# Decoder layer on one core: the moving tiles of the split matmuls start 32 or 96 bytes past a multiple of 128

## The reference

```
mod = (silu(c) @ w_ada + b_ada)                      # 9 vectors of 1024
h = modulate(rms_norm(x, g1), shift, scale)
x = x + 0.5 * gate * (silu(h @ w_gate) * (h @ w_up)) @ w_ffn1_out     # D_FF = 2816
h = modulate(rms_norm(x, g2), ...)
u_pool, q_lat, kv_lat, k_rope, g_pool, g_mla = split(h @ w_in)
br_pool = (causal pooling of u_pool, 4 windows) -> group product -> w_pool_proj
br_mla  = causal attention of 8 heads over low-rank q, k, v -> w_mla_proj
x = x + gate * ((sigmoid(g_pool) * br_pool + sigmoid(g_mla) * br_mla) @ w_out)
h = modulate(rms_norm(x, g3), ...)
x = x + 0.5 * gate * swiglu(h)                        # second FFN, as the first
```

## Time and profile before

| what | us |
|---|---|
| time, median of 3 (1081.8 to 1082.19) | 1082.01 |
| the profiled execution's own time | 1083.97 |
| its span, first to last instruction | 1082.1 |
| PE busy | 1050.4 |
| PE weight loads busy | 885.0 |
| DVE busy | 530.6 |
| ACT busy | 370.3 |
| POOL busy | 70.1 |

### The profile page before, as it was taken

How to read it: one execution, slowest core, us unless ns; L and a number is a source line. 1 busy time by engine, 2 the same in 40 slices (tenths; PEclk the granted TensorE clock), 3 DMA queues, 4 the chain that set the end, 5 groups by cost and what they waited for, 6 DMA issues and landing times.

```text
span 1082.1 us, 13106 instructions
## 1 busy us (share of the span) xinstructions
PE 1050.4 (97%) x5086; PEld 885.0 (82%) x5086; DVE 530.6 (49%) x718; ACT 370.3 (34%) x519; POOL 70.1 (6%) x56
## 2 busy tenths in 40 slices
PE   3999999999999999998999999999999999999998
PEld 2888888888888899897888887898888888888887
DVE  5765555564663274677565455474333333322221
ACT  6633232323222144574444443334232323222211
POOL 0000000000000000851000004200000000000000
PEclk9999999999999999998999999999999999999999
DMA  9765555554763322121121122322323222222222
GB/s 353 285 243 191 193 194 189 199 184 168 246 235 123 117 87 101 71 89 68 40 78 41 76 78 78 117 79 78 114 80 112 81 105 88 91 82 83 104 87 98
DMA packets 28878, 138.62 MB, mean 128 GB/s; under 512 B 3248, under 2 KB 3504, under 8 KB 21168
## 3 DMA queue, kind: packets, MB, share of 16 engines
q1 hardware_dynamic: 28848, 138.23, 35.3%
HBM read 136.12 MB, written 2.10 MB: 128 GB/s over the span
## 4 chain that ended last, share of the span: by engine, by line
PE 87%; DVE 5%; POOL 3%; ACT 2%; issue 1%; DMA 1%; SPq 1%; DVEq 0%; POOLq 0%; ACTq 0%
PE bank L450 28%; PE bank L451 27%; PE bank L452 27%; PE bank L794 2%; DMA ada_first<-w_ada 1%; POOL window L1947 1%; ACT w_hi L894 1%; DVE w_lo L1290 1%; PE bank L810 1%; DVE qk_tok L1533 1%; POOL u_pad L1953 1%; PE bank L776 1%; POOL window L1952 1%; POOL h L1976 0%; DVE mvar L1639 0%
## 5 line engine op out<-in xcount | busy, mean ns | idle before, releaser
L450 PE MATMUL bank<-h_hi,w_hi 128*128 128x512 f32 (+1 forms) x976 | 373.6, 383 | 3.7 <-DVE h_lo L1480 2.8
L451 PE MATMUL bank<-h_hi,w_lo 128*128 128x512 f32 (+1 forms) x976 | 370.8, 380 | 0.0
L452 PE MATMUL bank<-h_lo,w_hi 128*128 128x512 f32 (+1 forms) x976 | 370.7, 380 | 0.0
L1290 DVE TENSOR_TENSOR w_lo<-w_raw,w_hi 128x2048 fp32r<-128x2048 f32 (+3 forms) x94 | 192.9, 2052 | 159.6 <-ACT w_hi L894 159.6
L450 PEld LDWEIGHTS bank<-h_hi,w_hi 128*128 128x128 f32 x976 | 184.3, 189 | 41.0 <-DVE h_lo L1480 3.2
L452 PEld LDWEIGHTS bank<-h_lo,w_hi 128*128 128x128 f32 x976 | 184.2, 189 | 34.8
L451 PEld LDWEIGHTS bank<-h_hi,w_lo 128*128 128x128 f32 x976 | 184.3, 189 | 33.7
L894 ACT ACTIVATE w_hi<-w_raw 128x2048 fp32r<-128x2048 f32 (+3 forms) x94 | 160.9, 1712 | 113.8 <-PE bank L452 63.5
L450 PE MATMUL bank<-act_hi,w_hi 128*128 128x512 f32 (+1 forms) x374 | 141.2, 378 | 0.5 <-DVE w_lo L1290 0.5
L452 PE MATMUL bank<-act_lo,w_hi 128*128 128x512 f32 (+1 forms) x374 | 140.8, 377 | 0.0
L451 PE MATMUL bank<-act_hi,w_lo 128*128 128x512 f32 (+1 forms) x374 | 140.8, 377 | 0.0
(11 more groups left out here) (189 smaller groups left out, 912.0 us busy)
## 6 DMA issues: line engine op xcount, KB each, us to landing
w_raw<-w_ffn_in SPq DMA_DIRECT2D x41, 1024.0 KB, 4.8
ada_raw<-w_ada SPq DMA_DIRECT2D x56, 512.0 KB, 5.1
w_raw<-w_ffn_out SPq DMA_DIRECT2D x32, 704.0 KB, 4.0
w_raw<-w_mix SPq DMA_DIRECT2D x19, 1024.0 KB, 4.8
ada_first<-w_ada SPq DMA_DIRECT2D x16, 512.0 KB, 12.7
w_raw<-w_ffn_in SPq DMA_DIRECT2D x6, 512.0 KB, 12.7
w_raw<-w_mix SPq DMA_DIRECT2D x3, 896.0 KB, 4.4
x_tok<-x_rows SPq DMA_DIRECT2D x4, 512.0 KB, 6.6
```

The lines of the kernel that those rows point to most:

```text
L450: nc.tensor.matmul(dst, a_hi, b_hi, start=start, stop=False)
L451: nc.tensor.matmul(dst, a_lo, b_hi, start=False, stop=False)
L452: return nc.tensor.matmul(dst, a_hi, b_lo, start=False, stop=stop)
L1290: nc.vector.tensor_tensor(w_lo[slot][:, 0:size], w_raw[slot][:, 0:size], w_hi[slot][:, 0:size].bitcast(F32), ALU.subtract).then_inc(lo_don ...
```

## The change

Only addresses change. `h_hi` moves 32 bytes up, to 32928 (32 past a multiple of 128); `h_lo` moves to 49376 (96 past); everything behind it moves by exactly 128, so its place against a multiple of 128 stays: the weights at 0, `scaled` at 64. `act_hi` then gets 96 bytes more (137568, 96 past) and `act_lo` 160 more (182688, 32 past). The small tiles at the end of SBUF move by 256 more. `square_note`, a scratch tile of the first norm that shares the place of `h_lo`, moves with it. The instructions of every engine, their order and their waits are the same as before, row for row; line numbers in the changed file are 3 higher from the first of the edits on.

```diff
         x = place("x", [P, KD, S])
+        cursor[0] += 32
         h_hi = place("h_hi", [P, KD, S], F32R)
+        cursor[0] += 64
         square_note = [place(f"square_note{i}", [P, D], at=cursor[0] + 4 * D * i) for i in range(TOK)]
         h_lo = place("h_lo", [P, KD, S], F32R)
+        cursor[0] += 32
         w_raw = [place(f"w_raw{i}", [P, SLOT]) for i in range(2)]
...
-        act_hi = [place(f"act_hi{f}", [P, NF, S], F32R, at=act_at) for f in range(2)]
-        act_lo = [place(f"act_lo{f}", [P, NF, S], F32R, at=act_at + 4 * NF * S) for f in range(2)]
+        act_hi = [place(f"act_hi{f}", [P, NF, S], F32R, at=act_at + 96) for f in range(2)]
+        act_lo = [place(f"act_lo{f}", [P, NF, S], F32R, at=act_at + 4 * NF * S + 160) for f in range(2)]
...
-        spare = [96 * kib + phase_at]
+        spare = [96 * kib + 256 + phase_at]
```

## The result

| | before | after |
|---|---|---|
| time, median (runs) | 1082.1 us (4) | 1110.0 us (4: 1109.4 to 1111.8) |
| ratio | | 1.0253, 95% interval 1.0241 to 1.0265 |
| profiled execution, its span | 1083.97, 1082.1 | 1110.35, 1108.5 |

The account below looks back on a forecast made before the run. PE, busy 97% of the span, was taken as the bound, so only the matmul pitch could matter. Step 1, Step 2, step 3 and Step 4, each 0, summed to 0: forecast the median, 1082.0 us, range 1062 to 1096.

Parts of the forecast that it names:

- What bounds the kernel: PE, busy 97% of the span with few waits, so addresses can matter only through the distance between two matmuls.
- Step 1: Moving operands at 32 or 96, 4050 matmuls: taken as 0, between 54 us faster and 21.5 us slower.
- disturbed pitch: Pitch after the scores of a head, 0.232 before it falls to 0.2267; held all run, 21.5 us slower.
- The bounds: Limits over 4050 matmuls: 54 us faster if 13.3 ns each goes, 21.5 us slower if pitch stays at 0.232.
- Rival A: 13.3 ns per matmul is a turn of 128 bytes; half turns within triples gain 18 us, 1064; chance 0.20.
- Rival B: Moving and weight reads collide less at different residues: faster by 3.4 us (1078.6) up to 54 us (1028); chance 0.18.
- Rival C: Unaligned moving read takes one piece more: slower, first price 13.5 us (1095.5), 27 us for 64-byte pieces; chance 0.22.
- Step 2: Shifted h loaded as weights in the latent projection: 1.3 us won or as much lost, taken as 0.
- step 3: VectorE's writes of the shifted h_lo and act_lo: 5% more each would cost under 0.7 us, taken as 0.
- Step 4: Everything else moves by 128 or 384 bytes and keeps its place modulo 128, latent projection's moving weights included: 0.
- fixed share: 13.3 ns in each matmul beside its columns, read as a delay in supplying the array; 54 us over 4050 matmuls.

## Why the prediction was wrong

*What bounds the kernel* was right: only the pitch could move the time, nothing else did by a whole us, and the waits stayed as they were. "So many matmuls by a possible change" was the right sum.

*Step 1 failed*, in the value that I took. I took 0, since "a shift of addresses may be made good by a shift in time of a few ns which the steady state finds for itself". It wasn't made good: at the distances of the changed kernel the rhythm of 0.2267 was not found again in either stretch of 280 us, whereas before, after a mere disturbance in time, it returns within eleven matmuls. The row that I called nearest to the new state, the steady one, was as far from it as a row could be: in all the split products with 512 moving columns that the trace holds, moving tile and weights had the same place modulo 256, and the steady pitch described that one case. The nearest row was the disturbed pitch of 0.232, where the rhythm is absent. Step 1 measured 23.8 us for h, 6.6 for act and -0.7 for 256 columns by the steady pitches, and 26.4 in the span, in place of 0.

*The bounds were too low as well.* I had used that 0.232 as the worst case of step 1, 21.5 us, which would be 1103.5; and the range stopped before that, at C's first price. The 0.232 is a mean of steps of 0.22 to 0.24, not a worst case; h's distances cost 9.0 ns a matmul and act's 6.7, where the bound had 5.3.

*Rival A*, a turn of 128 bytes, is refuted: with high and low half a turn apart it had a gain of 18 us, and both kernels with such tiles were slower (1110.0 and 1098.4); 0 is not the slow case but the fast one. *Rival B* had it the wrong way round: equal places are what holds the fast rhythm. *Rival C* had the right sign and the wrong mechanism: the start by itself, at multiples of 32, costs nothing.

*Step 2*, h as stationary operand, and *step 3*, the writers, were priced at 0 and nothing came from them: the parts that PE's own pitch explains already make up the whole, and the writers' medians are 483, 692 and 693 ns after the change, against 483, 692 and 692. *Step 4* asked for places modulo 128 only. That was the blind spot of the whole argument. The latent projection, from which I read that multiples of 128 don't matter, has a pitch of 0.1117 both before and after the change, although the distances in it changed. Matmuls of only 128 columns are hardly faster (0.109 when the heads are turned), so something other than its columns seems to bound it, and there the distance doesn't show.

The prediction weighed the rule of the Trainium skill that PE has two independent read ports and that a weight load steals nothing from the running matmul ("TensorE: Matmul & The Clock Gate", part 2, step 1), and noted that the disturbed pitch was against it. The benches, with no other engine at work, show the same instructions at 226.7 to 237.7 ns by place alone, and a change of place between the two operands is enough; so where one is read does bear on the time of the other. How many ports there are, no run here shows. By the Trainium skill's rule of 16-byte lines ("SBUF — State Buffer", the box on cachelines) distances of 32, 64 and 128 bytes, all whole lines, would be alike; measured are 233.4, 228.9 and 233.3.

What stays open is the mechanism. The pitch of 226.7 is 256 + 16 cycles at 1.2 GHz, those of many other distances 280, and with 448 columns the order of the two turns round. It looks like two reads falling into step with a period, but that is a guess: no run here shows what the period belongs to, why distances other than 0 have more than one rhythm, nor why a block of 32 columns doesn't reach 213.

## What to carry to other kernels

When PE is the bound, give the moving tile and the weights of float32r products with 512 moving columns starts that are equal modulo 256, at multiples of 32, also when a pad or a small tile is put between them; in the kernels here other distances cost 2 to 9 ns in each of 3630 matmuls. For fewer moving columns measure it first: at 256 and 448 a distance of 128 was slightly better. A steady pitch that is exactly the same everywhere in a trace is a state that something holds; before pricing a change at nothing, ask what all these instances have in common and whether the change takes that away. And when a trace has one value of a parameter only, measure the others in a bench of a few us per case: its pitches foretold what three whole kernels lost to within 2 us.

## What the hardware showed unexpectedly

- The pitch of a split product with 512 moving columns depends on the distance of moving tile and weights modulo 256 bytes: 226.7 ns at 0, 228.9 at 64, 231.1 to 236.7 at most others. Moving tiles 4 bytes up cost 10 ns, 4 bytes down nothing.
- Off distance 0 the same addresses can have more than one steady pitch: 232.4 and 233.3 in the two FFNs of one kernel at distance 128.
- The fixed share is not made by the number of weight columns: 226.7 ns with 128, 231.7 with 32.
- At 448 and 256 moving columns a distance of 128 is slightly better than 0 (204.0 against 206.7, 118.7 against 120.0).
- At distance 0 the fast rhythm is found again within one to eleven matmuls, after a disturbance or a move of all four tiles.
